# Streaming encoder with a mixture of experts: the rows of the last two experts combined by products, attention's key preparation reordered

## What is computed

```python
def hier_moe(xn, w_group, b_group, w_expert, b_expert, w1, w3, w2):
    ...
    top_v, top_i = lax.top_k(le_sel, TOP_K)
    wts = jax.nn.softmax(top_v, axis=-1) * g_p
    e_idx = g_idx[:, None] * EXPERTS_PER_GROUP + top_i
    gates = jnp.sum(jax.nn.one_hot(e_idx, N_EXPERTS, dtype=jnp.float32) * wts[..., None], axis=1).astype(t.dtype)
    y = jnp.zeros_like(t)
    for e in range(N_EXPERTS):
        hdn = jax.nn.silu(t @ w1[e]) * (t @ w3[e])
        y = y + gates[:, e:e + 1] * (hdn @ w2[e])
    return y.reshape(shp)

def mla_latent(h, pos, kv_norm, w_dkv, kv_a_norm, k_rope_norm):
    c = rms_norm(h, kv_norm) @ w_dkv
    c_kv = rms_norm(c[..., :KV_RANK], kv_a_norm)
    ...

def mla_expand(c_kv, w_uk, w_uv, k_nope_norm):
    k_nope = rms_norm(jnp.einsum('blr,rhd->blhd', c_kv, w_uk), k_nope_norm)
    ...

def mla_query(xn, pos, w_dq, q_a_norm, w_uq, q_nope_norm, q_rope_norm):
    cq = rms_norm(xn @ w_dq, q_a_norm)
    ...
```

## Time and profile before

| | |
|---|---|
| device time, three runs | 1150.98, 1155.64, 1156.69 us; median 1155.64 |
| profiled execution: span, own time | 1156.9 us, 1158.54 us |
| busy share of the span | PE 91%, PEld 66%, DVE 67%, ACT 51%, POOL 6% |
| mean granted clock of PE | 0.949 |
| DMA rate while the experts run | 380 to 403 GB/s |
| chain that ended last | PE 87%, ACT 5%, DVE 4%, DMA 2% |
| layer 0: copy of the last expert's y on ACT | 553.54, 1.02 us |
| layer 0: the six gathers are issued | 558.84 to 565.16, one each 1.27 us |
| layer 0: last pass of DVE, the residual is complete | ends at 573.6 |
| attention: the last key sum ahead of the projections | 587.20, 3.62 us |
| attention: input of the residual's root on DVE; its root on ACT | 577.5; 588.01 |

### The profile page before, as it was taken

How to read it: one execution, slowest core, us unless ns; L and a number is a source line. 1 busy time by engine, 2 the same in 40 slices (tenths; PEclk the granted TensorE clock), 3 DMA queues, 4 the chain that set the end, 5 groups by cost and what they waited for, 6 DMA issues and landing times.

```text
span 1156.9 us, 13561 instructions
## 1 busy us (share of the span) xinstructions
PE 1049.8 (91%) x5117; PEld 759.9 (66%) x5117; DVE 777.7 (67%) x605; ACT 594.7 (51%) x453; POOL 66.8 (6%) x101
## 2 busy tenths in 40 slices
PE   5999999999999999999789877587989999999992
PEld 4889998796666666665566736475766666666651
DVE  4557563558888988986325544554768888888872
ACT  5336332343777777775232322223437777777750
POOL 5000000010000000000300100000030000000001
PEclk9999999978999999999899985889899999999996
DMA  9434432936999999992640003003579999999924
GB/s 354 156 120 151 162 117 91 417 147 222 382 389 380 401 393 392 403 395 79 234 134 1 35 0 146 1 1 160 204 275 352 381 385 402 388 387 401 393 89 174
DMA packets 44824, 280.27 MB, mean 242 GB/s; under 512 B 6289, under 2 KB 10673, under 8 KB 32097
## 3 DMA queue, kind: packets, MB, share of 16 engines
q1 hardware_dynamic: 33136, 240.21, 53.6%
q0 software_dynamic: 8960, 30.07, 7.7%
q10 hardware_dynamic: 2688, 9.44, 2.1%
HBM read 260.91 MB, written 19.09 MB: 242 GB/s over the span
## 4 chain that ended last, share of the span: by engine, by line
PE 87%; ACT 5%; DVE 4%; DMA 2%; issue 1%; ACTq 0%; POOL 0%; POOLq 0%; SPq 0%; DVEq 0%
PE ps L185 31%; PE ps L191 15%; PE ps L523 4%; PE ps L577 4%; PE ps L620 3%; PE ps L1796 3%; PE ps L1822 3%; PE ps L1218 2%; PE ps L583 2%; PE ps L531 2%; PE ps L1956 2%; PE ps L627 1%; PE ps L1187 1%; PE ps L1938 1%; PE ps L1012 1%
## 5 line engine op out<-in xcount | busy, mean ns | idle before, releaser
L1047 DVE TENSOR_TENSOR raw_lo<-raw,moe_wh 128x4096 fp32r<-128x4096 f32 x48 | 212.4, 4425 | 46.3 <-ACT moe_wh L1042 46.2
L1047 DVE TENSOR_TENSOR moe_wl<-moe_raw,moe_wh 128x4096 fp32r<-128x4096 f32 x48 | 212.3, 4425 | 35.1 <-ACT moe_wh L1042 35.0
L185 PE MATMUL ps<-moe_wh,moe_xh 128*72 128x512 f32 x512 | 204.7, 400 | 6.3 <-DVE moe_xl L1130 6.3
L185 PE MATMUL ps<-moe_wh,moe_xl 128*72 128x512 f32 x512 | 202.9, 396 | 0.0
L1042 ACT ACTIVATE moe_wh<-raw 128x4096 fp32r<-128x4096 f32 x48 | 173.8, 3620 | 7.6 <-PE ps L1947 3.9
L1042 ACT ACTIVATE moe_wh<-moe_raw 128x4096 fp32r<-128x4096 f32 x48 | 173.7, 3621 | 4.1 <-DMA moe_raw<-in_moe_w_dram 4.1
L185 PEld LDWEIGHTS ps<-moe_wh,moe_xh 128*72 128x72 f32 x512 | 73.2, 143 | 50.9 <-DVE moe_xl L1130 6.9
L185 PEld LDWEIGHTS ps<-moe_wh,moe_xl 128*72 128x72 f32 x512 | 73.1, 143 | 43.5 <-issue 1.1
L325 DVE TENSOR_TENSOR raw_lo<-raw,gm_wh 128x4096 fp32r<-128x4096 f32 x12 | 53.1, 4425 | 71.3 <-ACT gm_wh L319 69.1
L185 PE MATMUL ps<-moe_wh,moe_hTh 128*72 128x512 f32 x256 | 82.6, 404 | 5.1 <-DVE moe_hTl L1135 5.1
L185 PE MATMUL ps<-moe_wh,moe_hTl 128*72 128x512 f32 x256 | 81.6, 400 | 0.0
(11 more groups left out here) (356 smaller groups left out, 1569.1 us busy)
## 6 DMA issues: line engine op xcount, KB each, us to landing
raw<-in_moe_w_dram SPq DMA_DIRECT2D x48, 2048.0 KB, 11.1
moe_raw<-in_moe_w_dram SPq DMA_DIRECT2D x48, 2048.0 KB, 11.4
raw<-in_gm_w_in_dram SPq DMA_DIRECT2D x7, 2048.0 KB, 8.1
moe_yrows<-moe_rows ACTq DMA_DIRECT2D x32, 288.0 KB
raw<-in_gm_w_out_dram SPq DMA_DIRECT2D x4, 2048.0 KB, 7.3
moe_rows<-moe_xrows POOLq DMA_DIRECT2D x28, 288.0 KB, 9.7
raw<-in_gm_w_in_dram SPq DMA_DIRECT2D x2, 1024.0 KB, 11.1
at_cache<-in_cache_ckv_dram SPq DMA_DIRECT2D x2, 1024.0 KB, 10.4
```

Of the source, the lines that this page charges most:

```text
L185: nc.tensor.matmul(out[c], x(t, k), wh[:, k, c * 512:c * 512 + 512], start=start and k == 0 and x is xh, stop=False)
L1047: nc.vector.tensor_tensor(w_lo[slot], w_raw[slot], w_hi[hi][:].bitcast(F32), ALU.subtract).then_inc(wl_ready, 1)
```

## The change

1. The rows of experts 14 and 15 (KEPT = 2, SENT = 14) are no longer stored to `yrows`. After step 2 DVE (`keep_rows`) builds from `spot`, `wts` and the picks a gate-weighted 0/1 matrix for each, the weights `sent_w` of the rows that were stored, and gather indices `back_i` in which a kept row is replaced by one fixed row; PE transposes the matrices (`turn_kept`) after steps 3 and 4, DVE copies them to SBUF (`kept_columns`). In the tail PE multiplies them with the y rows in SBUF (`spread_y`) into six PSUM banks (SPREAD), and DVE adds these to `h`.
2. The gathers wait for the store of expert 13 and for the weights of the last expert to be free up to w_used 3*NE-5; they write to the raw weight slot and to two row buffers. `yrows` is filled at the start by four copies from HBM, so that the fixed row is finite.
3. Steps 3 and 4 of the experts are written out as well; the overflow loop uses banks BY and BY+1 alone.
4. Attention: W_uk, half of the cache, w_dkv, w_dq and the rest of the cache are loaded during the last expert; the W_uk transposes wait for two tiles of the residual, the keys for all three; keys 0 and 1 come before the projections, 2 and 3 behind them, then 4 to 7. ACT takes the residual's root before the squares of keys 0, and the root of the keys after squares 4; DVE takes the sums of keys 0 to 3 after the latent rows.

```diff
-        y_rows = [rows[:, i] for i in range(4)] + [spare[:, i] for i in range(2)]
+        def y_rows(l, i):
+            return raw[:, SLOT[l][0], i * D:(i + 1) * D] if i < 4 else rows[:, i - 4]
+        SPREAD = [(0, 1), (2, 3), (4, 7)]
...
+        def experts(eng, step, after=()):
+            for e in range(5):
                 step(e, e % 2, e // 2)
+                if e >= 2 and e - 2 < len(after):
+                    after[e - 2]()
...
         def moe_pool(g, l):
             if l == 0:
+                for r in range(0, ROWS, SEQ):
+                    n = min(SEQ, ROWS - r)
+                    g.dma_start(yrows[r:r + n], A["x_prompt"][0, 0:n, :]).then_inc(pad_written, 16)
...
+            g.wait_ge(rt_dst, 2 * l + 2)
             g.wait_ge(y_final, l + 1)
+            g.wait_ge(w_used, M_MOE[l] + 3 * NE - 5)
+            g.wait_ge(xT_done, NE * (l + 1))
...
-                    g.indirect_dma_start(y_rows[2 * t + k], None, yrows[0:SLOTS],
-                                         bass.IndirectOffsetOnAxis(ap=dst_i[:, TILES * k + t:TILES * k + t + 1], axis=0)
+                    g.indirect_dma_start(y_rows(l, 2 * t + k), None, yrows[0:SLOTS + 1],
+                                         bass.IndirectOffsetOnAxis(ap=back_i[:, TILES * k + t:TILES * k + t + 1], axis=0)
...
                 if is_last(e):
                     y_copy(e - 1, 1 - par)
-                    store_y(e - 1, 1 - par)
                     return
...
             y_copy(NE - 1, 1)
-            store_y(NE - 1, 1)
...
+            def keep_rows():
+                v.wait_ge(xT_done, E0 + KEPT)
+                own = spot[:, :, SENT:NE]
+                for i in range(KEPT):
+                    shape = [P, TILES, CAP]
+                    dve_link(v, nc.vector.tensor_tensor(hot[:, i], const[:, C_SLOT:C_SLOT + CAP].unsqueeze(1).to_broadcast(shape),
+                                                        own[:, :, i].unsqueeze(2).to_broadcast(shape), ALU.is_equal))
...
+                for i in range(KEPT):
+                    last = nc.vector.tensor_tensor(hot[:, i], hot[:, i], kept_w[:, :, i].unsqueeze(2).to_broadcast(shape), ALU.mult)
+                    last.then_inc(rt_hot, 1)
...
+                nc.vector.tensor_copy(back_i[:], dst[:]).then_inc(rt_dst, 1)
+            def kept_columns(i):
+                v.wait_ge(kept_T, KEPT * l + i + 1)
+                nc.vector.tensor_copy(kept_hot[:, i], ps[0:CAP, BR, 0:TOK]).then_inc(rt_hot, 1)
+            experts(v, step, [keep_rows, lambda: kept_columns(0), lambda: kept_columns(1)])
...
             for t in range(TILES):
                 v.wait_ge(y_back[t], 32 * (l + 1))
...
+            for t in range(TILES):
+                b0, b1 = SPREAD[t]
+                v.wait_ge(spread, TILES * l + t + 1)
+                nc.vector.tensor_tensor(h[:, t].rearrange("p (c n) -> p c n", c=2), h[:, t].rearrange("p (c n) -> p c n", c=2),
+                                        ps[:, b0:b1 + 1:b1 - b0], ALU.add).then_inc(combined, 1)
...
+            def spread_y(i, t):
+                for c in range(2):
+                    last = nc.tensor.matmul(ps[:, SPREAD[t][c]], kept_hot[:, i, t * P:(t + 1) * P],
+                                            rows[0:CAP, 2 + i, c * 512:c * 512 + 512], start=i == 0, stop=i == KEPT - 1)
+            experts(pe, step, [lambda: turn_kept(0), lambda: turn_kept(1)])
             transpose_hidden(NE - 1)
+            pe.wait_ge(rt_hot, 3 * KEPT * (l + 1))
+            pe.wait_ge(y_out, E0 + NE - 1)
+            spread_y(0, 0)
+            spread_y(0, 1)
             product_y(NE - 1, 3 * NE - 1, 2, 5)
+            spread_y(0, 2)
+            pe.wait_ge(y_out, E0 + NE)
+            for t in range(TILES):
+                spread_y(1, t).then_inc(spread, 1)
...
         def at_sync(sp):
+            sp.wait_ge(combined, TILES)
...
-                if t == 0:
-                    mean_squares(v, 0)
-            inverse_key_rms(v, 0)
...
             nc.vector.tensor_copy(c_sb[:, SAMPLE, KVR:], kr[:, SAMPLE]).then_inc(at_lat, 1)
+            mean_squares(v, 0)
+            inverse_key_rms(v, 0)
...
         def at_tensor(pe):
             pe.wait_ge(ld_cache[0], 48)
+            pe.wait_ge(combined, 2)
...
+            pe.wait_ge(combined, TILES)
+            for b in range(2):
                 prepare(b, b % 2)
...
+            for b in range(2, 4):
+                prepare(b, b % 2)
+            pe.wait_ge(ld_cache[1], 32)
             pe.wait_ge(ch_rms, 1)
```

More of the change, by code:

```diff
@@ L1629, in squares @@
             def squares(b):
-                if b % 4 == 0:
+                if b and b in LEADS:
                     cache_copies(b)
-                if b % 4 < 3:
+                if b and b + 1 not in ENDS:
                     cache_copies(b + 1)
@@ L1638, in squares @@
                     nc.scalar.activation(sqT[:, b % 2, i * 512:i * 512 + 512], ps[:, 2 + i], ACT.Square).then_inc(ch_sq, 1)
[L1640 to L1641 removed]
+            cache_copies(0)
+            cache_copies(1)
             root(a, stat[:, 1, 0:TILES])
+            squares(0)
+            squares(1)
             for t in range(TILES):
[L1644 to L1645 removed]
                 for i in range(2):
@@ L1801, in prepare @@
                         last.then_inc(ch_K, 1)
-                if b % 4:
+                if b not in LEADS:
                     sum_squares(b - 1, 1 - par)
-            for b in range(4):
+                if b + 1 in ENDS:
+                    sum_squares(b, par)
+            pe.wait_ge(combined, TILES)
+            for b in range(2):
                 prepare(b, b % 2)
-            sum_squares(3, 1)
             pe.wait_ge(ld_at, 32)
```

132 lines of the change are left out of this document (79 added, 53 removed).

## The result

The changed kernel takes 1209.62 us (median of 4 runs, 1208.28 to 1211.36), the kernel before 1156.16 (4 runs): a ratio of 1.0443, 95% interval 1.0405 to 1.0482. The forecast of 1160.3 us was wrong by 49 us, and the time lies 44 us above the upper end of its range, 1166. Nearly all of it lies in one place.

The account below looks back on a forecast made before the run. The prediction took TensorE, busy 91% of the span, as the bound. Experts +5.4, layer 1's tail -10.2, layer 0 into attention +9.5 and fills 0 gave +4.7 us, so 1160.3 us, range 1152 to 1166.

Parts of the forecast that it names:

- part 1: Experts, both layers: preparing kept rows delays DVE's operands for PE and adds six transposes; 2.7 us per layer, +5.4 in all.
- The rival on the clock: Experts: PE falls to half rate after each stop, 1.7 us a layer, 1163.7 us in all; chance 0.12.
- rows 9: Trace rows on PE's clock: kept after a stop of 1.53 us, at 0.51 over 3.5 us after one of 2.56.
- Kept rows in the experts: Experts: PE waits 1.5 us for moe_hTl, 2.0 with moe_xl, plus 0.7 of transposes; 2.7 us per layer.
- Tail of layer 1: End of layer 1: gathers covered, then DVE's overflow loop, six passes and three additions; end 1146.7 instead of 1156.9, -10.2 us.
- W_uk, +7.0: Layer 0 into attention: W_uk transposes start at 564.1, 7.0 us later, behind PE's new products and overflow loop.
- To the last key product, +9.5: Attention's first stretch in layer 0 ends at 665.0 instead of 655.5, +9.5 us; bounds +5.5 to +11.5.
- W_uk to the last sum: Attention, a sign: this stretch takes 101 us, 98.4 before; clearly under 98 would show the forecast wrong.
- Fills, 0: Start of the kernel: four GpSimd copies from HBM to HBM, 3.4 MB near a weight load; cost 0, bound +5.
- a delay behind them of up to 5 us as a rival: gMLP: fills hold up a weight load, ACT starts 5.2 us late, decisive from 3.4; 1165.5 us, chance 0.10.
- The rival of the short empty loops: Overflow loops: short when nothing is queued, 4.1 us off layer 1, 3.4 off layer 0; 1152.8 us, chance 0.07.
- The rival in which the residual gates attention: Layer 0 into attention: the residual, not PE's sum, is the bound, gaining 10.9 us; 1140 us, chance 0.06.

Follow-up runs that it names:

- the run with 104 products: Changed kernel with 104 PE products of 128 columns into a free bank ahead of the first group of kept-row transposes: 1206.19 us, ratio 1.0424.
- the kernel with the transposes later: Changed kernel with PE's two groups of kept-row transposes one step later, behind steps 3 and 4 instead of 2 and 3: 1162.59 us, ratio 1.0065.
- the run with the test: Against the kernel with the transposes later: empty overflow-loop rounds on ACT, DVE and PE put under one test of the count; 1157.07 us, ratio 1.0009.
- the keys' order: Against the kernel with the transposes later: attention keys 0 to 3 all ahead of the projections, as before the change; 1156.31 us, ratio 1.0003.

## Why the prediction was wrong, and where it was right

**The step that failed** is in part 1: "PE also gets 2 x 3 transposes of hot, 0.11 us each in a stream, 0.7 with the change of operand." The six transposes were priced as work and not as a wait. I took them to stand behind PE's steps 3 and 4, as the description of the change says too, and as DVE's copies do. But `experts` hands out its list from step 2 on, and PE's list has two entries where DVE's has three: PE's first group is behind step 2, level in number with the `keep_rows` that makes its operand. Equal numbers are not equal times. The trace of before had what was needed. DVE finishes its step 2 where moe_hTl of expert 2 starts, 326.33, and PE's first product of step 3, which follows its step 2, started 9.1 us ahead of that:

```profile
317.21 0.39 PE L185 MATMUL ps<-moe_wh,moe_xh 128*72 128x512 f32 x1
```

With the 2.9 us up to the second weighted matrix that is a stop of 12, and the run shows 11.9. For the second group the queue to read was the bank: one bank for both groups, so the copy between them, behind DVE's step 3, is a wait of PE too.

No rival held it. The rival on the clock ("PE falls to half rate after each stop in the experts", 1.7 a layer) had the mechanism that followed, behind stops that it did not have: 8.3 us in all, 1.4 to 2.7 after each of four, and the run with 104 products shows that it goes with the standing. Behind the forecast's own stop, the 1.25 us for moe_hTl, the clock stayed at 1.00 in both layers. But the premise taken from rows 9, that PE keeps its clock after a stop of 1.53 us, holds in some executions alone: behind the same stop of 1.53 us in layer 1 the clock stayed at 1.00 in the kernel before and fell to 0.50 for some 3 us in the changed kernel and in the one with the transposes later.

With that step mended, the other terms can be read from the kernel with the transposes later: forecast 1160.3, measured 1162.59, inside the range. Its four runs spread over 6.6 us, more than any term but the tail and attention, so the terms are better judged by their stages than by this total; where no kernel is named, the numbers are those of the changed kernel.

- Kept rows in the experts, 2.7 us per layer: 2.2 in each (from 0.7 to 2.9 us behind the kernel before across layer 0's experts, from 9.7 to 11.9 in layer 1). The wait for moe_hTl was 1.25, not 1.5, and the 0.5 behind it for moe_xl did not come.
- Tail of layer 1, -10.2: -10.7 from moe_xl of expert 15 to the end of the span (-11.0 to the last addition), with the order of events as forecast but for the gathers, which took twice as long to issue, under cover. What the forecast did not see is that PE's products end as late as DVE's passes. It had that number (1140.5 for the last tile against 1139.8 for the passes) and did not say that the loop could therefore be worth 1.8 us at most; the run shows 0.2.
- W_uk, +7.0: +6.4. To the last key product, +9.5: +8.6, with a stop of 2.89 us for 2.9 at the sums. W_uk to the last sum: 100.5 us (590.43 to 690.92) for 101. That the sum came so close is in part the clock's doing: in the kernel with the transposes later, where 6.8 us of that stretch were at 0.50 and not 17.1, it is +5.4, the forecast's lower bound, and W_uk to the last sum 97.6 us, under the 98.4 of before; a stretch clearly under 98 was to be a sign of being wrong.
- Fills, 0 with a delay behind them of up to 5 us as a rival: the delay was 8.9 us and the effect 0. The rival's point of decision, 3.37 us of cover, was too low; the next three copies and the next split had cover of their own.
- The rival of the short empty loops fell: DVE stood 5.53 us in its loop, for the 5.3 forecast. The Trainium skill's figures ("Advanced Engine Details and Errata", Control Flow Timing) give an estimate of 2.7 for it, too low by a factor of two here. The run with the test is in line with the measured price: the first pass came 5 us sooner.
- The rival in which the residual gates attention fell as well: attention's last key product was late by 8.6 us although the residual was 11.2 us early, both counted from moe_xl of expert 15.

What stays open: single versions differ by 2 to 5 us in ways that the stages of one profiled execution do not carry, since the clock falls at other places in each. So the gain of the keys' order and of the loops' test alone are known by direction at best, not to the microsecond.

## What to carry to other kernels

When an instruction is placed behind "step e" on one engine and its operand is made behind "step e" on another, look up when each of them ends that step in the trace: engines that run the same loop can stand half a step apart, and the price of a six-instruction addition may be that distance. Cost every added instruction on the bounding engine twice, as work and as a wait, with the time at which its last input is made, and take a shared bank or buffer for such an input. Where two chains end together, as DVE's passes and PE's products did, taking work from one is worth nothing until the other is shortened.
